# Splitting GpSimd's weight rounding into instructions of 256 columns

## The reference

```
h = x + W_out [ HGRN2(hn) || chunk-gMLP(hn) ],  hn = RMSNorm(x), one combined input projection
h = h + CrossAttn(RMSNorm(h), memory K/V)      (4 heads, 256 memory tokens)
h = h + W_down relu(W_up RMSNorm(h))^2
y = RMSNorm_final(h)
```

## Time and profile before

| what | value |
|---|---|
| time, median of 3 runs | 2955.88 us (2953.66 to 2956.56) |
| time of the profiled execution | 2955.48 us |
| its span, first to last instruction | 2953.7 us |
| mean granted TensorE clock | 0.992 |
| PE busy | 2889.2 us (98%) |
| DVE busy | 1273.9 us (43%) |
| ACT busy | 627.6 us (21%) |
| POOL busy | 484.3 us (16%), all of it before 842 us |

### The profile page before, as it was taken

The page is one execution under the profiler, slowest core; times in us unless marked ns, Lnnn a source line. Parts: engine busy times, 40 slices in busy tenths (PEclk is TensorE's granted clock), DMA queues, the critical chain, the costliest instruction groups (busy, mean ns, idle before and its releaser), DMA issues.

```text
span 2953.7 us, 40414 instructions
## 1 busy us (share of the span) xinstructions
PE 2889.2 (98%) x17203; PEld 2334.5 (79%) x17203; DVE 1273.9 (43%) x2093; ACT 627.6 (21%) x967; POOL 484.3 (16%) x389
## 2 busy tenths in 40 slices
PE   7998899999999999999999999999999999999998
PEld 6786788777888888778888888887778888877787
DVE  5679733444343833322243744222334483322223
ACT  4423221201013411110112422110002341111011
POOL 0197505788830000000000000000000000000000
PEclk9999999999999999999999999999999999999999
DMA  8795657998975455666566455676767545567654
GB/s 289 279 339 199 243 188 248 348 326 282 331 281 185 147 188 193 239 209 214 202 213 238 152 171 182 197 252 229 293 223 286 185 145 192 178 226 280 241 188 152
DMA packets 207676, 675.92 MB, mean 229 GB/s; under 512 B 22864, under 2 KB 28240, under 8 KB 207504
## 3 DMA queue, kind: packets, MB, share of 16 engines
q1 hardware_dynamic: 200480, 662.72, 64.3%
q10 hardware_dynamic: 7024, 10.68, 1.0%
HBM read 542.84 MB, written 130.48 MB: 228 GB/s over the span
## 4 chain that ended last, share of the span: by engine, by line
PE 88%; DVE 10%; ACT 1%; DMA 1%; issue 0%; POOL 0%; ACTq 0%; SPq 0%; DVEq 0%; POOLq 0%
PE half L913 79%; DVE lvl L2149 3%; PE half L921 2%; PE half L1235 2%; DVE lvl L2162 2%; PE half L1047 1%; PE half L930 1%; DVE bn L2218 1%; PE half L1115 1%; PE half L1245 0%; DVE ends L2157 0%; DVE state L2198 0%; DMA w_pairs<-stage 0%; DVE stats L2245 0%; PE half L1103 0%
## 5 line engine op out<-in xcount | busy, mean ns | idle before, releaser
L913 PE MATMUL half<-a_hi,w_ring 128*128 128x512 f32 x2560 | 822.9, 397 | 0.1
L913 PE MATMUL half<-w_ring,a_hi 128*128 128x512 f32 x2176 | 678.1, 393 | 0.0
L913 PE MATMUL half<-w_ring,ht_hi 128*128 128x512 f32 x2016 | 626.6, 392 | 0.0
L913 PEld LDWEIGHTS half<-a_hi,w_ring 128*128 128x128 f32 x2560 | 480.2, 188 | 132.4 <-issue 15.1
L913 PE MATMUL half<-a_lo,w_ring 128*128 128x512 f32 x1280 | 505.4, 395 | 0.0
L913 PEld LDWEIGHTS half<-w_ring,a_hi 128*128 128x128 f32 x2176 | 411.0, 189 | 90.7
L913 PEld LDWEIGHTS half<-w_ring,ht_hi 128*128 128x128 f32 x2016 | 378.9, 188 | 82.5
L913 PE MATMUL half<-w_ring,a_lo 128*128 128x512 f32 x1088 | 434.4, 399 | 3.1 <-DVE a_lo L1778 2.4
L913 PE MATMUL half<-w_ring,ht_lo 128*128 128x512 f32 x1008 | 395.4, 392 | 0.4 <-DVE ht_lo L2368 0.4
L2376 DVE SCALAR_TENSOR_TENSOR x<-half,rstd,x 128x512 f32<-128x512 f32 x252 | 171.8, 745 | 301.1 <-PE half L913 301.1
L844 POOL TENSOR_TENSOR w_ring<-w_raw,zero 128x512 fp32r<-128x512 f32 x192 | 230.3, 1199 | 341.4 <-PE half L930 134.5
(11 more groups left out here) (300 smaller groups left out, 2408.3 us busy)
## 6 DMA issues: line engine op xcount, KB each, us to landing
w_ring<-w_pairs SPq DMA_DIRECT2D x704, 512.0 KB, 3.3
w_pairs<-w_ring SPq DMA_DIRECT2D x192, 512.0 KB, 5.0
w_pairs<-stage SPq DMA_DIRECT2D x16, 1024.0 KB, 4.9
w_raw<-in_w_up SPq DMA_DIRECT2D x64, 256.0 KB, 4.7
w_raw<-in_w_down SPq DMA_DIRECT2D x64, 256.0 KB, 4.0
w_s<-in_w_up SPq DMA_DIRECT2D x8, 2048.0 KB, 11.9
w_s<-in_w_down SPq DMA_DIRECT2D x8, 2048.0 KB, 11.3
w_raw<-in_w_in SPq DMA_DIRECT2D x48, 256.0 KB, 4.0
```

Source lines behind the costliest of these rows:

```text
L913: m = nc.tensor.matmul(ps[:, j, :], l, r, start=(i == 0 and q == 0), stop=(i == tiles_in - 1 and q == 2))
```

## The change

POOL does each of the two steps in two instructions of 256 columns: the two halves of the rounding, then the wait, then the two halves of the remainder. Only the second half of each step signals. Nothing else is changed.

```diff
-                nc.gpsimd.tensor_tensor(w_hi[:, k, :], w_raw[:, s, :], zero[:].to_broadcast([P, 512]),
-                                        ALU.add).then_inc(w_rounded, 1)
+                for c in (slice(0, 256), slice(256, 512)):
+                    m = nc.gpsimd.tensor_tensor(w_hi[:, k, c], w_raw[:, s, c], zero[:].to_broadcast([P, 256]), ALU.add)
+                m.then_inc(w_rounded, 1)
                 pool.wait_ge(w_rounded, g * RING + (n + k + 2))
-                nc.gpsimd.tensor_tensor(w_lo[:, k, :], w_raw[:, s, :], w_hi[:, k, :].bitcast(F32),
-                                        ALU.subtract).then_inc(w_split.sem, 1)
+                for c in (slice(0, 256), slice(256, 512)):
+                    m = nc.gpsimd.tensor_tensor(w_lo[:, k, c], w_raw[:, s, c], w_hi[:, k, c].bitcast(F32), ALU.subtract)
+                m.then_inc(w_split.sem, 1)
```

## The result

The changed kernel takes 2964.97 us (median of 9 runs, 2960.83 to 2966.68), the one before 2955.88 in the same comparison: a ratio of 1.0032, interval 1.0023 to 1.0041. It is 9.1 us slower; the forecast was 2962 (2946 to 2977). The profiled execution took 2963.38 us with a span of 2961.6, against 2953.7: 7.9 us.

What follows compares the result with a forecast made beforehand. PE, busy 2889.2 of 2953.7 us, was taken as the bound, waiting on DVE, which POOL blocks. Terms 1.3 - 1.3 + 8.0 + 0.5 + 0.8 - 3.1 + 0.6 = +6.8 us on 2955.5 gave 2962 (2946 to 2977).

Steps and rivals of the forecast that it cites:

- The rule of the wait: Where POOL and DVE block each other: exactly one DVE instruction passes per POOL instruction; a step falls from 1.31 to 0.82 us.
- A half alone: Undisturbed POOL: halves of 0.62 and 0.75 us, 0.20 not halving, a tile 2.69 us, 0.32 more than now.
- 151.8 to 228.7: Stretch in us before the level-product stage: POOL's lead goes, PE ends zq 4.3 us later, the stage begins 1.3 us later.
- POOL's deficit under L2162: Just before the stage: PE loses about 2 us to POOL's slow tiles under DVE's L2228 and L2162.
- Units 0 and 1: First two units of the level-product stage: unit 0 -1.3 us; unit 1 +8.0, all its 17 DVE instructions blocked by POOL's backlog.
- Units 2 to 7: Later units of the stage: +0.5 and +0.8 in units 2 and 4, 3 unchanged, -3.1 in 5, +0.6 in 6.
- The projections: Up and down projection, 128 tiles: POOL's busy time grows by 41 to 356 us of 380, hidden under PE.
- the 0.52 of the prediction: Added POOL time in us a tile from which, in the projections, the cover goes and the excess falls on PE.
- The halves nearly cancel: Rival: savings in units 0 and 5 match unit 1's loss, or PE's standing time hides it; 2952 to 2961; chance 0.24.
- Shorter blocks win: Rival: in the stage from 228.7 us halves block no more than 25 DVE instructions; 2940 at best, or 2948; chance 0.17.
- POOL the bound: Rival: a half keeps 0.42 us fixed, a tile takes 3.13, PE waits before 228 us and in projections; about 2986; chance 0.11.

Runs made afterwards that it cites:

- halves_from_40: Kernel before, with halves only for tiles 40 to 63, whole instructions for tiles 0 to 39 and the projections: 2953.73 us against 2954.62, ratio 0.9997.
- gate7: Kernel before, whole instructions, with POOL waiting ahead of tile 48 for unit 7's level products: 2951.11 us against 2955.29, ratio 0.9987.
- gate6: Kernel before, whole instructions, with POOL waiting ahead of tile 48 for unit 6's level products: 2956.21 us against 2955.29, ratio 1.0000.
- halves_last: Kernel before, with halves only for the 128 tiles of the up and down projections, whole for tiles 0 to 63: 2959.11 us against 2954.62, ratio 1.0016.
- halves_short: Changed kernel, with two sample-token weight products (zig, zuv) loading a quarter of their rows, timing only: 2961.28 us against the kernel before's 2955.29, ratio 1.0017.

## Why the prediction was right, and where it erred

The mechanism (DVE waits less each time, POOL falls behind, unit 1 pays) was right, and each size up to the end of unit 1 within 2 us. The closeness of the total is partly luck: one later step and the projections were wrong.

**The rule of the wait** held everywhere. From single starts and ends in the traces: fourteen L2149 per instruction take 1.32, 0.825, 0.845 and 0.58 us beside POOL instructions of 512, 256, 508 with 4, and 128 columns, one for one.

**A half alone.** Predicted 0.62, 0.75 and 2.69 us a tile; measured 0.61, 0.74 and 2.65. The fixed part, by the two sizes, is 2 x 0.61 - 1.04 = 0.18 us, predicted 0.20. The estimate after the GPSIMD Engine Reference (Trainium skill, section 3.1), 0.23, was somewhat high.

**151.8 to 228.7.** Predicted: the lead gone, zq's end late by 4.3 us (measured 212.91 against 209.96, from a tile 4 that was 0.6 earlier: 3.6; the prediction's own terms, 4.9 less 0.9, give 4.0 and not 4.3), DVE's gain lost in the wait for zq (16.59 us), and the stage 1.3 us late. Measured from tile 4 the stage comes 0.5 us earlier (74.0 against 74.5), not 1.3 us later: zq's delay was set 0.7 us and POOL's deficit under L2162 about 1 us too high.

**Units 0 and 1.** Predicted 16.4 and 17.4 us, measured 15.5 and 17.9, from 17.7 and 9.4. The 8 us of unit 1 were the largest term and the right one, and halves_from_40, where they are missing, and POOL's timeline in unit 1 bear out the backlog.

**Units 2 to 7: the mechanism was missed, the sum met by luck.** Predicted +0.5, 0, +0.8, -3.1 and +0.6 for units 2 to 6 and nothing beyond; measured -3.6, +5.5, -0.1, -9.6, -1.9, and +8.7 between unit 7 and tile 48: -1.0 in all where -1.2 was forecast. The step that failed is "Unit 5 has a burst of six tiles that blocks it almost to the end": it kept the burst where it was. SP's queue ties it to tile 43. The raw tile 47 is loaded once tile 43 is split; behind it stand some fifty small loads and two large ones for the sample tokens, and only then the raw tile 48. SP's timeline before, then after:

```profile
265.72 0.33 SPq L604 DMA_DIRECT2D w_raw<-in_w_in  x1
...
286.25 0.50 SPq L604 DMA_DIRECT2D w_raw<-in_w_out  x1
```

```profile
277.78 0.33 SPq L604 DMA_DIRECT2D w_raw<-in_w_in  x1
...
298.16 0.50 SPq L604 DMA_DIRECT2D w_raw<-in_w_out  x1
```

20.5 and 20.4 us between them. POOL's backlog made this pair 12 us late, and the burst with it. POOL's timeline at tile 48, before, then after:

```profile
299.92 1.04 POOL L844 TENSOR_TENSOR w_ring<-w_raw,zero 128x512 fp32r<-128x512 f32 x1 [7.60 <-DMA w_raw<-in_w_out]
```

```profile
312.06 3.96 POOL L845 TENSOR_TENSOR w_ring<-w_raw,zero 128x256 fp32r<-128x256 f32 x2 [7.81 <-DMA w_raw<-in_w_out]
```

It left unit 5 (-9.6) and fell on unit 6 and on DVE's work behind it (vv, L2208, which takes 8.39 us and took 5.05, then uu), for which PE then waits 8.3 us (+8.7). gate7 and gate6 make both halves of this with whole instructions. The prediction said that SP's queue "only sees POOL's times move"; that a moved time can move a burst by a unit was not followed through. Had the burst stayed, -3.1 was a fair estimate: halves_from_40 has -4.4. The +5.5 us of unit 3 and the -3.6 of unit 2 look like the same thing: POOL did tiles 41 to 44 in unit 2 before (258 to 268 us), and most of 42 to 46 in unit 3 after (275 to 288 us). No experiment took these two apart.

**The projections.** "315.0 us busy ... +0.32 x 128 = 41 gives 356, hidden under PE" is the other step that failed. It compared busy time with the whole 380 us. The added time was right, the cover was not. POOL's waits from 460 to 865 us, before, then after:

```profile
POOL w_ring L844 <- DMA w_raw<-in_w_up: 126.2, 6, 96.6
POOL w_ring L844 <- PE half L913: 24.1, 32, 2.6
```

```profile
POOL w_ring L845 <- DMA w_raw<-in_w_up: 121.5, 6, 92.3
POOL w_ring L845 <- PE half L915: 0.2, 1, 0.2
```

From the start of tile 96 to the end of tile 223 POOL took 378.8 us before: 24.1 waiting for PE, 29.6 waiting for raw tiles (126.2 - 96.6), 325.1 its own. After, it took 397.6: 0.2, 29.2 and 368.2. Its own time grew by 43.1 us, 0.34 a tile, where 0.32 was forecast. What could cover that was the 24 us of waiting for PE and 16 us of lead (tile 223 was ready 18.3 us ahead of PE before, 2.3 after): 40 us, 0.31 a tile, and not the 0.52 of the prediction. The gaps for raw tiles can't be used. Three of them (tiles 120, 136 and 200, 21 us) stand behind 2 MB loads for the sample tokens, one (tile 104, 8 us) where SP's queue itself waits before the next block's gain row. The rest, some 3 us, and the 1.0 us of waiting for tile 224 make the 3.7. halves_last (385.4) bears out the added time, halves_short (381.5) the gaps. The lead, 16 us at tile 96, is down to 0.5 us at tile 200.

The total came close because two misses have opposite signs: the stage was set 2 us too high (+6.8 for +4.8) and the projections 4 us too low.

**The rivals.** The halves nearly cancel: not so, 9.1 us (6.8 to 12.1 by the interval) are beyond the 5.9 that this rival allows. Shorter blocks win: not so. DVE is 29.5 us less busy, but what it gains before 228 us goes into its wait for zq, and in the units it meets more, shorter blocks in other places. The rule from SBUF — State Buffer (Trainium skill, Who interferes with whom), that whoever starts first keeps the pair for the whole instruction, agrees with the traces for each block; it says nothing of how many blocks follow, and that decided here. POOL the bound: true for tiles 12 to 28, whose lead is under 1 us in the changed kernel's trace, and for the last 24 tiles, but not at this rival's price.

## What to carry to other kernels
When one engine blocks another for an instruction at a time, count the instructions, not only their length: cutting them in two shortens each wait (here from 1.32 to 0.825 us) but doubles the number, and the fixed cost (0.14 us for each added instruction here) delays the helper that the bound engine needs. To see whether a helper has room, add the time in which it can't work for lack of input to its busy time. And before changing the instructions, look at where the helper's bursts fall; two waits that moved one burst by 23 us gave 9.4 us, more than any cutting did.

## What the runs showed of the hardware that was not expected
The blocking depends on who is running. In a stream of POOL instructions, each lets exactly one DVE instruction by, even one of 4 columns. A POOL instruction that comes while DVE streams back to back waits until DVE's whole run is over. In the changed kernel a single POOL instruction of 256 columns takes 8.20 us in place of 0.61; DVE's run beside it starts at 293.97 us and ends with this L2269, at 301.70:

```profile
293.98 8.20 POOL L845 TENSOR_TENSOR w_ring<-w_raw,zero 128x256 fp32r<-128x256 f32 x1 [6.09 <-PE half L915]
```

```profile
299.42 2.28 DVE L2269 TENSOR_TENSOR vn<-vn,lnb_row 128x2048 f32<-128x2048 f32 x1
```

And the scan (128x128, with ones and the data in SBUF) is blocked like the two-operand instructions: 16 take 5.16 us with POOL idle, 20.03 beside whole POOL instructions, and 11.95 beside halves.
